# A two-layer hybrid inference step: projection by token tile with the norm behind it, longer rows for the expert weights, and edits at the start

## What is computed

```python
sh1, sc1, g1, sh2, sc2, g2 = modulation(silu_cond, w_mod, b_mod)      # one set for context, one for latent tokens
h = rms_norm(x, norm1) * (1 + sc1) + sh1
merged = sigmoid(g_attn) * (attn @ w_br_attn) + sigmoid(g_hgrn) * (rec @ w_br_hgrn)   # attention and recurrence of h @ w_in
x = x + g1 * (merged @ w_out)
h = rms_norm(x, norm2) * (1 + sc2) + sh2
scores = sigmoid(h @ w_router)                                        # 16 experts, best group of 4, best 2 in it
act = silu(h @ w_gate[e]) * (h @ w_up[e])                             # (1024, 512) each
x = x + g2 * sum over the two experts of weight * (act @ w_down[e])   # (512, 1024)
```

## Time and profile before

| | us |
|---|---|
| median of three runs | 1604.6 (1602.77 to 1606.4) |
| the profiled execution | 1598.92 |
| its span, first to last instruction | 1597.1 |
| TensorE busy | 1401.8 (88%) |
| VectorE, ScalarE, POOL busy | 519.8, 335.0, 240.2 |
| mean rate of the DMA engines | 220 GB/s |

### The profile page before, as it was taken

One profiled execution on the slowest core, in us unless ns is written; L12 is line 12 of the kernel. 1 busy time (PEld: TensorE's weight loads), 2 busy tenths in 40 slices (PEclk: granted clock), 3 DMA queues, 4 the chain that ended last, 5 costly groups with the idle time before them and its releaser, 6 DMA issues.

```text
span 1597.1 us, 18517 instructions
## 1 busy us (share of the span) xinstructions
PE 1401.8 (88%) x7179; PEld 768.5 (48%) x7180; DVE 519.8 (33%) x1041; ACT 335.0 (21%) x495; POOL 240.2 (15%) x213
## 2 busy tenths in 40 slices
PE   4699999899998899989965999988999598999882
PEld 1365545656554444544423655566654344444441
DVE  1333423744113411121125344278311521111114
ACT  1105533651101100100101065265100100001010
POOL 2260003841000000000012600186100000000001
PEclk9899999999999899999986999999999899999996
DMA  9635453176424999996984331211414444999994
GB/s 344 246 109 189 181 208 109 53 253 261 158 106 150 363 380 396 399 339 248 398 304 156 109 106 54 106 53 53 145 53 158 184 166 177 339 396 397 396 395 178
DMA packets 157043, 351.96 MB, mean 220 GB/s; under 512 B 5880, under 2 KB 13128, under 8 KB 156992
## 3 DMA queue, kind: packets, MB, share of 16 engines
q1 hardware_dynamic: 138208, 314.48, 53.0%
q0 software_dynamic: 6576, 22.80, 4.0%
q10 hardware_dynamic: 12208, 13.98, 2.6%
HBM read 335.69 MB, written 15.55 MB: 220 GB/s over the span
## 4 chain that ended last, share of the span: by engine, by line
PE 71%; DVE 10%; SPq 7%; DMA 6%; ACT 3%; issue 2%; POOL 0%; DVEq 0%; ACTq 0%; POOLq 0%
PE pG L1401 21%; PE pS L1481 10%; PE pG L1393 9%; SPq L472 6%; PE pG L1496 5%; PE pG L1623 5%; PE pG L1489 4%; DMA ring<-in_w_mod_dram 2%; PE pX L1322 2%; PE pX L1481 2%; DVE ring L1005 2%; PE pG L1355 2%; DMA ring<-in_w_exp_up_dram 1%; DVE modb L1007 1%; PE pX L1447 1%
## 5 line engine op out<-in xcount | busy, mean ns | idle before, releaser
L1401 PE MATMUL pG<-hT,ring 128*128 128x384 f32 x896 | 299.5, 488 | 1.6 <-ACT gen L842 1.6
L1481 PE MATMUL pS<-ring,gen 128*64 128x256 f32 x2048 | 229.8, 381 | 11.5 <-DMA ring<-in_w_exp_up_dram 9.5
L1401 PEld LDWEIGHTS pG<-hT,ring 128*128 128x128 f32 x896 | 168.0, 191 | 115.5 <-issue 4.7
L1481 PEld LDWEIGHTS pS<-ring,gen 128*64 128x64 f32 x2048 | 148.1, 138 | 100.5 <-issue 19.2
L1393 PE MATMUL pG<-ring,hT 128*128 128x512 f32 (+1 forms) x384 | 150.0, 548 | 1.4 <-DVE hT L964 0.7
L1496 PE MATMUL pG<-ring,gen 128*64 128x512 f32 x512 | 116.9, 598 | 5.2 <-DVE gen L1278 5.2
L1273 DVE TENSOR_TENSOR gen<-pS,gen 128x256 f32<-128x256 f32 x32 | 13.6, 425 | 313.4 <-PE pS L1481 313.4
L1393 PEld LDWEIGHTS pG<-ring,hT 128*128 128x128 f32 x384 | 72.6, 192 | 72.1 <-issue 67.7
L660 POOL DMA_INDIRECT gen<-y_scr,idx x12 | 11.8, 985 | 628.5 <-ACTq L892 625.5
L1489 PE MATMUL pG<-hrow,gen 128*64 128x512 f32 x408 | 95.4, 603 | 2.2 <-DVE gen L1173 1.5
L871 ACT COPY gen<-pG 128x512 f32<-128x512 f32 x32 | 18.8, 586 | 348.6 <-PE pG L1496 348.6
(11 more groups left out here) (276 smaller groups left out, 1655.8 us busy)
## 6 DMA issues: line engine op xcount, KB each, us to landing
ring<-in_w_exp_up_dram SPq DMA_DIRECT2D x32, 2048.0 KB, 20.4
ring<-in_w_exp_down_dram SPq DMA_DIRECT2D x32, 2048.0 KB, 19.2
ring<-in_w_exp_gate_dram SPq DMA_DIRECT2D x32, 2048.0 KB, 18.3
ring<-in_w_mod_dram SPq DMA_DIRECT2D x24, 2048.0 KB, 9.4
ring<-in_w_in_dram SPq DMA_DIRECT2D x20, 2048.0 KB, 8.4
modb<-mod_scr POOLq DMA_DIRECT2D x20, 512.0 KB, 9.2
y_scr<-gen ACTq DMA_DIRECT2D x72, 128.0 KB, 5.5
ring<-in_w_out_dram SPq DMA_DIRECT2D x4, 2048.0 KB, 10.1
```

The costliest lines, as they stand in the source:

```text
L1401: ins = pe.matmul(ps[:, 0:TOK], w[:, k, c0:c0 + P], src[:, k, :], start=(k == 0), stop=(k == nk - 1))
L1481: ins = pe.matmul(dst[64 * hf:64 * hf + 64, 0:256], x[:, k, :], w[:, k, 256 * hf:256 * (hf + 1)], start=(k == 0), stop=(k == KC - 1))
```

## The change

- **Projection and second norm.** The groups of `w_out` run tile by tile (`i, t = n % 2, n // 2`), and each tile's square, root, scale and shift follow its second group. The transposes of tiles 0 and 1 stand behind groups 4 and 5, the logits of each tile are products of their own, and those of tile 2 are last. `mergedT` moves to slot 4 of the ring (`mergedS`), as `hrow` is now written while the projection runs. The second norm's row is written in another order: channel 8 c + k in column 128 k + c.
- **Longer rows.** Gate, up and router weights are read with channel 8 p + k in partition p, 16 KB in one row; down with rows of 8 KB. To match, VectorE writes its product with a pairwise step (`by_pairs`).
- **Start.** Zeroing `y_scr` moves from ACT to SP, behind unit ff of layer 0; the norm weight and x are loaded behind mod 0 instead of mod 1, the small tensors behind mod 3; the masks come as uint8, without a cast.
- **Modulation.** Two bias instructions lie in each of the four column groups; the sum of an odd unit lies in columns 32 to 63.
- `norm_scale` of the second norm stands ahead of the projection.

```diff
-    return kind, NT * (i + 1) - 1 if kind == "wo" else LAST_GROUP[kind]
+    return kind, 2 * (NT - 1) + i if kind == "wo" else LAST_GROUP[kind]
...
+        mergedS = S[:, 0:KC * TOK].rearrange("p (j t) -> p j t", j=KC)
...
-                    src = a[("w_exp_gate", "w_exp_up")[part]][L, e, :, :].rearrange("(k p) n -> p k n", p=P)
+                    src = a[("w_exp_gate", "w_exp_up")[part]][L, e, :, :].rearrange("(p k) n -> p (k n)", p=P)
...
-                    src = a["w_exp_down"][L, e, :, :].rearrange("(k p) n -> p k n", p=P)
+                    src = a["w_exp_down"][L, e, :, :].rearrange("(a p c) n -> p a (c n)", a=2, p=P)
...
                     unit(L, name)
+                    if (L, name) == (0, ("ff", 0)):
+                        sp.wait_ge(zeroed, 1)
+                        for i, r in enumerate(range(NE * BLK, YROWS, P)):
+                            sp.dma_start(y_scr[r:r + P, :].rearrange("p (a c) -> p a c", a=4),
+                                         bc(zeros, [P, 4, 256], 1)).then_inc((*e_ydma, v_dma)[i % 3], 16)
...
+            pool.wait_ge(landed[0], 16)
             load_norm(0, 0)
-            pool.wait_ge(landed[1], 16)
...
+            pool.wait_ge(landed[3], 16)
             for n, (dst, name, w) in enumerate(((qnw, "q_norm_w", HD), (knw, "k_norm_w", HD), (hnw, "hgrn_norm_w", HK))):
...
-            pool.dma_start(masks32, a["masks"]).then_inc(small_in, 16)
+            pool.dma_start(masks[:, :, :].rearrange("p s t -> p (s t)"), a["masks"]).then_inc(small_in, 16)
...
-                mean_root(ms_done, 2 * L + 2, 0, NT, rstd_done)
+                for t in range(NT):
+                    mean_root(ms_done, (NT + 1) * L + t + 2, t, 1, rstd_done)
...
+            def norm2(L):
+
+                for t in range(NT):
+                    act.wait_ge(x_mid, 2 * NT * L + 2 * t + 2)
+                    act.activation(hrow[:, t, :], xs[:, t, :], ACT.Square,
+                                   accum_out=stat[:, t:t + 1]).then_inc(sq_done, 1)
+                    if t > 0:
+                        hT_half(2 * L + 1, t - 1)
...
+            def norm2(L, t):
+                dve.wait_ge(sq_done, NT * (2 * L + 1) + t + 1)
+                dve.tensor_scalar(stat[:, t:t + 1], stat[:, t:t + 1], 1.0 / D, EPS, ALU.mult,
+                                  ALU.add).then_inc(ms_done, 1)
+                dve.wait_ge(rstd_done, (NT + 1) * L + t + 2)
+                h = hrow[:, t, :].rearrange("p (k c) -> p c k", k=KC)
+                x, scale, shift = (v.rearrange("p (c k) -> p c k", k=KC)
+                                   for v in (xs[:, t, :], modb[:, 1, min(t, 1), :], modb[:, 0, min(t, 1), :]))
+                link(dve.scalar_tensor_tensor(h, x, stat[:, t:t + 1], scale, ALU.mult, ALU.mult))
+                dve.tensor_tensor(h, h, shift, ALU.add).then_inc(h_ready, 1)
...
                     dve.tensor_tensor(x, x, wo_tmp[:, n % 2, :], ALU.add).then_inc(x_mid, 1)
-                norm(L, 1)
+                    if n >= 2 * (NT - 1):
+                        hT_half(2 * L + 1, i)
+                    if i == 1:
+                        norm2(L, t)
+                hT_half(2 * L + 1, NT - 1)
...
-                for j in range(4):
-                    r = 4 * (m % MODS) + j
-                    ins = pe.matmul(ps[0:32, P * j:P * (j + 1)], ident[:, r:r + 1].broadcast_to([P, 32]),
-                                    brow[:, m // MODS, :], start=False, stop=(j == 3))
+                for q in range(4):
+                    r = 4 * (m % MODS) + q
+                    ins = pe.matmul(ps[32 * q:32 * q + 32, P * q:P * (q + 1)], ident[:, r:r + 1].broadcast_to([P, 32]),
+                                    brow[:, m // MODS, :], start=False, stop=True)
...
-                finish_group(pe.matmul(ps[0:32, :], const[:, C_SEL:C_SEL + 32], mod_parts(m),
+                r = 32 * (m % 2)
+                finish_group(pe.matmul(ps[r:r + 32, :], const[:, C_SEL:C_SEL + 32], mod_parts(m),
...
                     finish_group(ins)
+                    if n >= 2 * (NT - 1):
+                        norm_turn(2 * L + 1, i)
+                logits(L, 0)
                 if L == 0:
                     mod(MOD_LATE)
                     mod(MOD_LATE + 1)
-                norm(L, 1)
...
+                logits(L, 1)
+                norm_turn(2 * L + 1, NT - 1)
+                logits(L, NT - 1).then_inc(rt_log, 1)
```

More of the change, by code:

```diff
@@ L765, in _ @@
                         mod_copy(m)
-                norm(L, 0)
+                norm1(L)
                 for h in range(HH - 1):
@@ L848, in _ @@
                     act.activation(gs[:, j % 2, :], ps[:, 0:TOK], ACT.Sigmoid).then_inc(gh_ready, 1)
[L849 removed]
+                norm2(L)
                 if L == 0:
@@ L1272, in _ @@
                         dve.wait_ge(e_silu, n + 2)
-                        dve.tensor_tensor(actb, bank[3][:, 0:256], gsil, ALU.mult).then_inc(e_act, 1)
+                        dve.tensor_tensor(by_pairs(actb), pairs(bank[3][:, 0:256]), pairs(gsil),
+                                          ALU.mult).then_inc(e_act, 1)
                         dve.wait_ge(e_gather, m + 2)
@@ L1296, in _ @@
                                 dve.wait_ge(v_act, b + 1)
-                                dve.tensor_tensor(act_o, bank[7][:, 0:256], gsil_o, ALU.mult).then_inc(v_dve, 1)
+                                dve.tensor_tensor(by_pairs(act_o), pairs(bank[7][:, 0:256]), pairs(gsil_o),
+                                                  ALU.mult).then_inc(v_dve, 1)
                                 dve.wait_ge(v_pe, b * 5 + 7)
@@ L1402, in cols, with norm_turn, logits @@
                 finish_group(ins)
-            def norm(L, which):
-                n = 2 * L + which
-                for t in range(NT):
-                    pe.wait_ge(h_ready, NT * n + t + 1)
-                    for hf in range(2):
-                        for c in range(4):
-                            k = 4 * hf + c
-                            ins = transpose(bank[2 + 2 * t + hf][:, P * c:P * (c + 1)], hrow[:, t, P * k:P * (k + 1)])
-                        ins.then_inc(hT_made, 1)
-                pe.wait_ge(hT_v, NT * (n + 1))
-                pe.wait_ge(hT_a, NT * (n + 1))
+            def norm_turn(n, t):
+                pe.wait_ge(h_ready, NT * n + t + 1)
+                for hf in range(2):
+                    for c in range(4):
+                        k = 4 * hf + c
+                        ins = transpose(bank[2 + 2 * t + hf][:, P * c:P * (c + 1)], hrow[:, t, P * k:P * (k + 1)])
+                    ins.then_inc(hT_made, 1)
+            def logits(L, t):
+                pe.wait_ge(hT_v, NT * (2 * L + 1) + t + 1)
+                pe.wait_ge(hT_a, NT * (2 * L + 1) + t + 1)
+                for k in range(KC):
+                    ins = pe.matmul(bank[2][0:NE, P * t:P * (t + 1)], wr[:, k, :], hT[:, k, P * t:P * (t + 1)],
+                                    start=(k == 0), stop=(k == KC - 1))
+                return ins
             def att(L, k):
@@ L1522, in _ @@
                     mod_broadcast(MOD_FIRST - 1)
-                norm(L, 0)
+                for t in range(NT):
+                    norm_turn(2 * L, t)
+                pe.wait_ge(hT_v, NT * (2 * L + 1))
+                pe.wait_ge(hT_a, NT * (2 * L + 1))
                 w = unit_in(L, ("q", 0))
@@ L1627, in _ @@
                     mod(MOD_LATE + 1)
-                norm(L, 1)
-                for k in range(KC):
-                    ins = pe.matmul(bank[2][0:NE, 0:TOK], wr[:, k, :], hT[:, k, :], start=(k == 0), stop=(k == KC - 1))
-                ins.then_inc(rt_log, 1)
+                logits(L, 1)
+                norm_turn(2 * L + 1, NT - 1)
+                logits(L, NT - 1).then_inc(rt_log, 1)
                 if L == 0:
```

90 lines of the change are left out of this document (44 added, 46 removed).

## The result

| | before | after |
|---|---|---|
| median | 1605.5 (1602.77 to 1606.59) | 1554.24 (1551.65 to 1557.46) |
| the profiled execution | 1598.92 | 1551.65 |
| its span | 1597.1 | 1549.8 |
| TensorE busy | 1401.8 | 1383.5 |

The ratio is 0.9684, 95% interval 0.966 to 0.9708: 51 us faster by the medians, 47 by the two profiled executions. I had said 1568, from 1557 to 1583.

The account below looks back on a forecast made before the run. TensorE was taken to bind mostly, with full DMA engines at the start, in layer 0's routing and the last experts. Savings of 11.5 + 2.5 + 8 + 4.5 + 10 = 36.5 us gave a 1568 us median, range 1557 to 1583.

Parts of the forecast that it names:

- the bound by loads in layer 0: Before expert 0's block: its up weights, issued at 535.31, land at 552.9, leaving 4.1 us to save.
- Layer 0: Output projection to expert 0: saves 4.5 us (2.5 to 8), capped by loads of expert 0's up weights.
- The third point: Third sign expected: in layer 0, TensorE waits for up weights of expert 0, where it waits for none now.
- my 11.7: Layer 0, projection to expert 0: saving on TensorE's path, 8.8 us as in layer 1 plus 1.8 and 0.9 from sums.
- Start: Up to the first projection: 4.0 MB and fewer following units ahead of mod 3's load save 11.5 us (7.9 to 14).
- Modulation units: Bias matmuls spread over column groups, and sums in different groups: together 2.5 us saved (0 to 6).
- Layer 1: Projection to logits: norm and logits of tiles 0 and 1 overlap other work; 8.0 us saved (4 to 9.3).
- whole 2.5: Second norm's writes with a step of 128: both instructions of the last tile doubled, +2.5 us; 1.2 was taken.
- Expert loads: Expert loop of layer 1: longer rows load faster and cut waits for weights; 10 us saved (0 to 11.2).
- Rival (a): Expert loads: row length is worth nothing, so 25 us remain saved, 1579 us; chance 0.22.
- rival (c): Expert loads: long rows read in lockstep collide in memory and the rate falls; 1646 us at a 20 us step; chance 0.04.
- (b): Whole kernel, rival: column groups side by side, whole start, no step cost; 1558 us; chance 0.14.

Follow-up runs that it names:

- order_back: The changed kernel with the output projection by column half again and norm, transposes and logits after all six groups: 1581.11 us, ratio 0.9855.
- rows_2kb: The changed kernel with the experts' rows as before (2 KB for gate and up, 4 KB for down): 1566.64 us, ratio 0.9764.
- warm: The changed kernel with added identity matmuls, results unread, in TensorE's holes of the routing (9 or 16 behind the logits' transposes): 1554.49 us, ratio 0.969.
- the bench: Separate kernel of only expert weight loads, by row length, and VectorE instructions, by step; 2 MB loads ran at 387 to 431 GB/s.

## Why the prediction missed

Of the 14 us between 1568 and 1554.24 the first pair of traces has 4.8 in the start, 4.1 in layer 0, 1.8 in the modulation units and 0.4 each in layer 1 and the expert loop; 3.1 lie in the step to the median, and two stages for which nothing was forecast make -1.9 and 1.3. The steps that failed are the bound by loads in layer 0, whose issue I held fixed, and the sizes of two terms, the start's following units and the bias.

**Layer 0 (4.5 forecast, 8.6 in the first pair of traces, 9.6 between the means).** The bound by expert 0's weights is real, but two steps of its sum were wrong. "It can't start earlier" held the issue of the up weights to mod 23's place in the projection. It hangs on TensorE finishing mod 22, which lies behind the logits, and so it moved 11 us with them; order_back shows it moving back. And "Longer rows (below) give back 1.5" counted bytes only: rows_2kb has the gate landing 5.1 us later, with SP held 21 us. The third point, "TensorE waiting for up weights of expert 0 where it waits for none now", didn't come; the gate arrived 1.4 us early. warm shows that the waits do appear once TensorE is some 3 us faster. So TensorE's own path and the loads now end together. The terms of my 11.7 for TensorE's path alone add up to 11.5, and the path gave about 11 of them if the gather is counted at one clock: it took 5.33 us after the change, 2.80 in the first trace of before and 4.71 in the second, whose stage was 10.5 us longer than after's. So the low clock behind the logits is not new with the change; the first trace of before happened to be without it in the gather and the block.

**Start (11.5 forecast, 15.7; 16.3 in the first pair).** The method held, one term was too small. 5.2 MB less were moved ahead of mod 3. The 4.0 that I took out are right: 3.15 in ACT's queue, 0.86 in POOL's (3.01 to 2.15). But I had added 1 us, 0.4 MB, for following units that no longer slip ahead, and SP's queue moved 1.2 MB less (10.34 to 9.14), 3 us. Mod 3 started 14.1 us earlier. The rest of the first pair is TensorE's: mod 3 took 1.92 us where it had 3.43, and its eight bias products 0.40 where they had 1.04. "Mod 3's landing near 35" was 32.4, "the first projection near 55" 50 to 52. Of the two prices inside, the zeroing cost 6.8 to 7.5 (7.9 by its bytes).

**Modulation units (2.5 forecast, 4.0 at the first `wo` group of layer 0).** This is a term I sized by the wrong row. "If the groups run side by side, 0.22" was the answer, and it stood in the text as one end; I took the value next to L1447's twelve products at 89 ns each, because both are short; what limits those twelve, no run tells, but it isn't what limits the bias. Eight units give 5.3, not 1.4. The 0.8 for the sums failed the other way: 1.81 us against 1.78. By 260 us of the kernel before 5.1 us were saved; 1.6 went right behind, where sixteen matmuls took 3.48 us at a granted clock of 0.57 (255.60 in after) that took 1.95 before. The second execution of after has such a spell elsewhere, in its first projection groups (33.15 us for 31.21), so I take it for spread and not for a cost of the edit.

**Layer 1 (8.0 forecast, 8.5).** Right, also inside: one turn between the groups, logits of tiles 0 and 1 in the hole, no group waiting for VectorE, the logits of a tile 1.92 us and thus at the high clock. The strided writes cost 1.4 for the last tile (2.00 and 1.91 against 1.29 and 1.22), where I took 1.2 and bounded 2.5. The low clock came behind the logits, in the positions, the gather (4.94 us) and the first block (8.81), as it had before the change (4.76 and 8.81), not in the turn.

The Trainium skill ("SBUF — State Buffer", section "Door 1: The DMA port swizzle") says that each access on a new 16-byte line pays. The bench agrees: two floats apart is free, four or more apart takes 2.0 us instead of 1.28. The page gives no size, and my "whole 2.5" took it for a doubling, which it isn't: it is a factor of 1.6.

**Expert loads (10 forecast, 10.2).** Right by a sum with two errors that cancel. The rate rose from 396 to 427 GB/s, so an expert's 6.55 MB need 15.3 us and not the 15.75 that I worked out; the loop's 12 steps then fall behind by 7 us, less than the cushion of 10.5, and all waits are gone. That is the upper end, which I put at 11.2 and which measured 10.2: the six waits and the end gave 11.5, and the two steps with further blocks took 1.0 longer. That 10 came out is luck. Rival (a), row length worth nothing, is refuted by rows_2kb, and rival (c) by the bench, where longer rows were faster throughout.

The Trainium skill ("DMA: Bandwidth & Descriptors", section "Why small descriptors are slow (HBM only)") has three fixed cycles a packet, by which 387 GB/s at 2 KB would become 403 at 16 KB. The bench has 431: the fixed part is 9.6 ns, two and a half times the 3.8 ns that three of 67 cycles make of an 85 ns row.

**The range.** Its low end was (b), the sum of the cheap sides, 14, 6, 9.3, 6 and 11.2. Two of these were passed (15.7 and 9.6), the others fell a little short. I had given (b) 0.14 and had taken a middle value in four terms of five, as if that were the cautious side; here each middle was too low or just right. Another 3 us of the miss are in the step from the profiled execution to the median: I carried over the 5.7 us of before, and after's median lies 2.6 above its profiled execution.

## What to carry to other kernels

When a bound is set by a transfer, follow its issue back to the semaphore that releases it: if this is work of the very engine that the change speeds up, the bound moves along. Price a queue's long descriptor lists also by what they hold up behind them: 21 us of SP's time here, on top of the bytes. And where a change leaves two resources ending together, test them together: in layer 0 earlier loads gave nothing, filling TensorE's holes 1.1 us, and both 5.2. Then look at the places where only one of the two can act, here layer 1, before the whole gain is put down to the pair.

## What the runs showed of the hardware

- Loads of 2 MB in rows of 2, 4, 8 and 16 KB run at 387, 410, 423 and 431 GB/s: 9.6 ns for a row and 75 for each 2 KB, per engine.
- Small matmuls in four different column groups of TensorE run side by side: eight of 128 columns in 0.22 us instead of 0.88. Two sums of 512 columns in different groups take 1.05 us (run warm, 514.64) if both inputs are ready, where two in one group took 1.95 (before, 234.56), both at the high clock.
- VectorE on 128x1024 float32: 1.22 to 1.29 us contiguous or with a step of two, 1.9 to 2.06 with a step of 4, 8 or 128, written or read.
- With matmuls whose result nobody reads in TensorE's holes of 1 to 5 us, the gather of 12 instructions ran at the higher of the two levels, in 2.8 us instead of 4.9 to 5.3. With nine of them in layer 1's hole of 4.8 us the positions began no later (59.4 us behind the first `wo` group, as without); sixteen of 256 columns there cost 2.2.
- A 2 MB load in 2 KB rows held SP for up to 5.3 us at its issue in the bench (11.06 to 32.4 us), and for 19.2 in rows_2kb behind other loads; one in 16 KB rows held it for 0.6 us at most in the bench.
